# Modulation tiles moved between stages of a two-block transformer kernel, and fewer products for the second layer

## What is computed

```python
ctx_out = l < DEPTH - 1
m_lat = (silu_c @ w_mod[l] + b_mod[l]).reshape(Bsz, N_MOD, 1, D)
m_ctx = (silu_cc @ w_mod[l] + b_mod[l]).reshape(N_MOD, D)
x = x + 0.5 * m_lat[:, 2] * swiglu(modulate(rms_norm_2(x), m_lat[:, 0], m_lat[:, 1]), ffn_in[l, 0], ffn_out[l, 0])
...
x = x + m_lat[:, 5] * o_lat
x = x + 0.5 * m_lat[:, 8] * swiglu(modulate(rms_norm_2(x), m_lat[:, 6], m_lat[:, 7]), ffn_in[l, 1], ffn_out[l, 1])
if ctx_out:
    ctx = ctx + m_ctx[5] * o_ctx
    ...
```

## Time and profile before

| | |
|---|---|
| median of 3 runs | 2531.78 us (2530.11 to 2533.71) |
| the profiled execution | 2532.84 us, its span 2531.1 us |
| mean granted TensorE clock | 0.977 of full speed |
| PE busy | 2378.8 us, 94% |
| DVE busy | 1468.0 us, 58% |
| ACT busy | 919.6 us, 36% |
| first block | 0 to 484 us of the span |
| feed-forwards (0,0), (0,1), (1,0), (1,1) | from about 493, 1394, 1780 and 2322 us; some 350 to 385 us each, the last about 200 |
| layer 0's mixer and recurrence | about 865 to 1375 us |

### The profile page before, as it was taken

How to read it: one execution, slowest core, us unless ns; L and a number is a source line. 1 busy time by engine, 2 the same in 40 slices (tenths; PEclk the granted TensorE clock), 3 DMA queues, 4 the chain that set the end, 5 groups by cost and what they waited for, 6 DMA issues and landing times.

```text
span 2531.1 us, 43473 instructions
## 1 busy us (share of the span) xinstructions
PE 2378.8 (94%) x18326; PEld 1997.6 (79%) x18326; DVE 1468.0 (58%) x2431; ACT 919.6 (36%) x1582; POOL 76.5 (3%) x148
## 2 busy tenths in 40 slices
PE   8999899999999998887878999999999999999998
PEld 6678768788888776676766888888888888778997
DVE  5565566665555576767564655545655553575553
ACT  2341133432322447643324533222523222455542
POOL 0000000000000000000000000000000000000000
PEclk9999999999999999987989999999999999999999
DMA  8236525544444321000003344444344443213553
GB/s 308 100 103 231 183 100 178 171 133 150 144 148 154 124 84 51 1 3 4 21 4 117 109 150 139 144 143 166 118 148 150 142 151 124 87 34 103 183 185 130
DMA packets 55920, 311.01 MB, mean 123 GB/s; under 512 B 5936, under 2 KB 9392, under 8 KB 28080
## 3 DMA queue, kind: packets, MB, share of 16 engines
q1 hardware_dynamic: 32944, 224.75, 25.8%
q0 software_dynamic: 20736, 75.51, 9.1%
q10 hardware_dynamic: 2048, 7.98, 0.8%
HBM read 307.16 MB, written 1.05 MB: 122 GB/s over the span
## 4 chain that ended last, share of the span: by engine, by line
PE 80%; DVE 11%; ACT 5%; issue 3%; DVEq 0%; DMA 0%; ACTq 0%; SPq 0%
PE bank L1641 16%; PE bank L1648 16%; PE bank L1644 16%; PE bank L1464 5%; PE bank L1461 2%; PE bank L1523 2%; PE bank L1539 2%; PE bank L1737 2%; PE bank L1048 2%; PE bank L1275 1%; PE bank L1282 1%; PE bank L1278 1%; PE bank L1351 1%; PE bank L1583 1%; PE bank L1410 1%
## 5 line engine op out<-in xcount | busy, mean ns | idle before, releaser
L2774 DVE TENSOR_TENSOR w_lo<-ring,w_hi 128x1024 fp32r<-128x1024 f32 (+1 forms) x195 | 232.3, 1193 | 398.9 <-ACT w_hi L2224 398.9
L1641 PE MATMUL bank<-ffn_x_hi,w_hi 128*128 128x512 f32 x984 | 383.0, 389 | 0.0
L1644 PE MATMUL bank<-ffn_x_lo,w_hi 128*128 128x512 f32 x984 | 382.8, 389 | 0.0
L1648 PE MATMUL bank<-ffn_x_hi,w_lo 128*128 128x512 f32 x984 | 382.8, 389 | 0.0
L2224 ACT ACTIVATE w_hi<-ring 128x1024 fp32r<-128x1024 f32 (+1 forms) x195 | 200.2, 1028 | 275.5 <-PE bank L1644 242.4
L2692 DVE SCALAR_TENSOR_TENSOR ms<-mod_rows,c_silu 128x1024 f32<-128x1024 f32 x200 | 244.0, 1220 | 1.7
L1641 PEld LDWEIGHTS bank<-ffn_x_hi,w_hi 128*128 128x128 f32 x984 | 184.7, 188 | 38.7 <-DVE w_lo L2774 0.6
L1648 PEld LDWEIGHTS bank<-ffn_x_hi,w_lo 128*128 128x128 f32 x984 | 184.7, 188 | 38.3
L1644 PEld LDWEIGHTS bank<-ffn_x_lo,w_hi 128*128 128x128 f32 x984 | 184.7, 188 | 38.3
L1641 PE MATMUL bank<-ffn_h_hi,w_hi 128*128 128x512 f32 x484 | 190.2, 393 | 0.0
L1648 PE MATMUL bank<-ffn_h_hi,w_lo 128*128 128x512 f32 x484 | 188.3, 389 | 0.0
(11 more groups left out here) (523 smaller groups left out, 4975.7 us busy)
## 6 DMA issues: line engine op xcount, KB each, us to landing
ring<-in_stream SPq DMA_DIRECT2D x211, 1024.0 KB, 4.9
mod_rows<-in_mod_stream POOLq DMA_DIRECT2D x144, 512.0 KB, 3.8
one_const<-in_one ACTq DMA_DIRECT2D x1, 1665.0 KB, 13.5
mix_const<-in_two ACTq DMA_DIRECT2D x1, 1440.0 KB, 6.2
win_const<-in_win ACTq DMA_DIRECT2D x1, 1216.0 KB, 5.4
x<-in_x SPq DMA_DIRECT2D x4, 256.0 KB, 4.7
c_silu<-in_c SPq DMA_DIRECT2D x1, 1024.0 KB, 10.1
x<-in_x SPq DMA_DIRECT2D x1, 1024.0 KB, 26.0
```

What stands on the lines that cost most here:

```text
L1641: mm = pe.matmul(bank[:, 0:tok], w_high, hi, start=k == 0, stop=False)
L1644: mm = pe.matmul(bank[:, 0:tok], w_high, lo, start=False, stop=False)
L1648: mm = pe.matmul(bank[:, 0:tok], w_low, hi, start=False, stop=last)
L2774: V.tensor_tensor(low[:, 0:h.nk, :], raw_half(h), high[:, 0:h.nk, :].bitcast(F32), ALU.subtract).then_inc(sem("w_split"), 1)
```

## The change

The first block keeps 5 tiles in each layer instead of 11 (four beside v, one beside the embedding). The rest go to the four feed-forwards: 22, 19, 17 and 4 tiles. For vectors 5 to 8 of layer 1, the instructions for context tokens (parts 1 and 3) are left out, and bias and scale are applied to the latent column alone. DVE waits once more in layer 0's mixer, for its own last head norms.

```diff
-MOD_BLOCK_ONE = ([True] * 4 + [False, True, True, False] + [True, True, True, False] + [True, True, False, False]) * 2
-MOD_FFN = [True] * FF_IN_PAIRS + [False, True] * 5 + [True, False]
-MOD_PLAN = MOD_BLOCK_ONE + MOD_FFN + MOD_FFN + MOD_FFN[:-2]
-MOD_AFTER_SCAN = sum(MOD_BLOCK_ONE + MOD_FFN)
+MOD_BLOCK_ONE = ([True] * 4 + [False] * 4 + [True] + [False] * 7) * 2
+MOD_FFN = ([True] * FF_IN_PAIRS + [True] * 11 + [False], [True] * FF_IN_PAIRS + [False, True, True] * 4,
+           [True] * FF_IN_PAIRS + [False, True] * 6, [True] * 4)
+MOD_PLAN = MOD_BLOCK_ONE + sum(MOD_FFN, [])
+MOD_AFTER_SCAN = sum(MOD_BLOCK_ONE + MOD_FFN[0])
+assert sum(MOD_PLAN) == 2 * MOD_TILES
...
+            def layer_ends(layer, v):
+
+                return 1 if layer == 1 and v >= 5 else 2
+
...
-                    link(V.scalar_tensor_tensor(products[:].rearrange("p a b -> p (a b)"), mod_rows[:, part // 2, :], 1.0,
-                                                c_silu[:, part % 2, :], ALU.mult, ALU.mult, accum_out=dst))
+                    if part % 2 == 0 or layer_ends(layer, j // 4) == 2:
+                        link(V.scalar_tensor_tensor(products[:].rearrange("p a b -> p (a b)"), mod_rows[:, part // 2, :], 1.0,
+                                                    c_silu[:, part % 2, :], ALU.mult, ALU.mult, accum_out=dst))
...
-                done = modv[:, layer, v]
-                link(V.tensor_tensor(done, done, param("b_mod", 72 * layer + KC * v, KC).unsqueeze(2).broadcast_to([P, KC, 2]), ALU.add))
+                n = layer_ends(layer, v)
+                done = modv[:, layer, v, :, 0:n]
+                link(V.tensor_tensor(done, done, param("b_mod", 72 * layer + KC * v, KC).unsqueeze(2).broadcast_to([P, KC, n]), ALU.add))
...
+                if layer == 0:
+                    dve.wait_ge(sem("heads_plain"), 6)
                 last_unit = (1, 3, 5, 7) if layer else (3, 7, 9, 11)
```

## The result

The changed kernel takes 2540.89 us (median of 12 runs, 2536.48 to 2549.23); the kernel before, run beside it on the same chip, 2533.46 us (12 runs, 2528.91 to 2538.56). The ratio is 1.0032, with a 95% interval of 1.0019 to 1.0045: slower by 8.1 us (4.8 to 11.4) by the ratio, by 7.4 us in the medians. The forecast was 6.3 us. All ratios and medians here are of executions in the fast state; two executions of the kernel before that ran beside those of question 5 and the doubled tile took 5332 and 6996 us and are left out. The profiled execution of the changed kernel took 2536.48 us, its span is 2534.7 us.

A forecast was written before the change was run, and what follows sets the result against it. TensorE was taken as the bound (busy 94% of the span), VectorE's queue order setting only feed-forward ends and norm entries. Terms 0 + 0 + 0 + 0 + 6.3 + 0 gave +6.3 us, a median of 2538.1 us; range 2533.0 to 2543.0.

The forecast's parts named there:

- Part 5, the halt: End of feed-forward (0, 1): four products in the last slot delay the addition to x; TensorE halts 5.0 us (4.8 to 5.04).
- Part 5, the clock: Behind that halt: TensorE's work up to the second sum runs at lowered clock, 1.3 us more, at most 1.86.
- Parts 1 to 4: First block's relief, added head-norm wait, fewer instructions in (1, 0), fuller output halves of (0, 0) and (0, 1): 0 each.
- part 2: VectorE's added wait for its own head norms ahead of the multiplication by z: 0, or 0.22 us if uncovered.
- Part 1: First block: twelve tiles, 59 us of VectorE, leave; covered by TensorE's projections, so 0, at most 8.0 us gained.
- Part 6: Feed-forward (1, 1): four tiles, eight instructions, and row loads, hidden by 2.7 us in hand: 0, at most 10.1 us.
- A: End of (0, 1): the clock stays up and only the queue counts, +5.0 us, 2536.8 us; chance 0.15.
- B: First block gives back 2.7 us of lowered clock and waiting, so +3.6 us, 2535.4 us; chance 0.15.
- C: Faster: four instructions at the end of (0, 1) hidden, first block gives 8.0 us back, 2523.8 us; chance 0.05.
- D: (1, 1) falls behind as ACT and VectorE miss the 11.52 us round: up to 10.1 us more, 2548.2; chance 0.15.

The follow-up runs named there:

- question 5: Three runs: kernel before without layer 1's last context products, 2533.7 us; changed kernel with them kept, 2554.44; kernel before with twelve first-block tiles' products doubled, 2555.01.
- the doubled tile: Changed kernel with tile 50's four products, in the last slot of feed-forward (0, 1), done twice: ratio 1.0056 to the kernel before.
- the run with TensorE kept busy: Changed kernel with seven unneeded TensorE products of 384 columns in front of the sum at the end of (0, 1): 2536.86 us, ratio 1.0017.
- the run with twice the products there: Changed kernel with the context products of layer 1's last four vectors kept, so four products a group in (1, 1): 2554.44 us, ratio 1.0079.
- the one-multiplication kernel: Changed kernel with tile 50 one slot earlier and one unused 128x1024 VectorE multiplication in the last slot's place: ratio 1.0009 to the kernel before.

## Why the prediction was right, and where its sizes were off

**Verdict.** Slower was forecast and is what came; 2538.1 us stands against 2540.9, inside the range. Of the 2.8 us between them 1.7 are the kernel before, which itself ran at 2533.46 us beside these runs and not at 2531.78. The mechanism is the one named, at its place: four products between two splits, a wait of 4.86 us at the sum (4 to 5 said), lowered clock behind it, and the rest as before to within about 0.5 us.

**Part 5, the halt:** 5.0 us taken, 4.86 measured; 5.2 of the loss with the clock kept up. Right within the bounds said for the wait (4.8 to 5.04).

**Part 5, the clock:** this is the term that was mis-sized. I took 1.3 us, no more than the 1.86 us up to the second sum; it is 3.1, and part 5's sum of 6.3 us, bounded at 6.9, measured 8.3. Up to the second sum the two sums came 1.73 us further apart, so nearly all of that stretch ran slowly, not two thirds of it; that alone lies inside the bound of 1.86. Then I said that behind the second sum TensorE has room. It does not: the third group of sums is itself on the path to the norm, and a second fall slowed it, for 1.2 us that the sum put at nothing. That one shouldn't be put down to the change entirely, since it also stands in three profiles with little or no halt.

The Trainium skill (page "TensorE: Matmul & The Clock Gate", Terms) takes throttled time times one minus the ratio. From the four stretches above this is 5 x (0.50 + 0.17 + 0.15 + 0.19) = 5.05 us, where the run with TensorE kept busy gives 3.1: the trace doesn't agree, as it didn't in the earlier trace rows, and for the same reason, part of the low time is idle. Its sum in the prediction, 8.4 us, came nearer to the result than mine, but with a figure of another stretch that counted idle time and knew of no second fall: that was luck.

**Parts 1 to 4:** 0 each was taken, and the starts move by 0.2 us in all for the first block and (0, 0), within the 1 us said. The wait added in part 2 shows nowhere. Two small steps were overlooked by all six parts: some 0.3 us between 925 and 1000 us in layer 0's mixer, and some 0.25 us between 1380 and 1700 us. They stand in all ten profiles of kernels with the new places of the tiles and in none of the three with the old, so they are the change's. With the first goes, in the changed kernel from 865 to 1000 us, a wait of TensorE that the kernel before doesn't have there:

```profile
PE bank L1353 <- DVE mix_in_q L3032: 0.2, 1, 0.2
```

What makes them is open. Part 1 had a bound of 8 us of gain; none came.

**Part 6:** 0, and nothing new in the waits of (1, 1). It was the nearest call (2.7 us in hand, 2.3 used), and the run with twice the products there shows that the margin was read rightly, to 0.1 us of wait, though not what the waits cost (11.9 us, 8.7 expected).

**Rivals.** A (the clock stays up, +5.0) is excluded in all profiles with this halt; kept busy by hand, the kernel behaves as A said. B and C (something back from the first block) found nothing: its starts moved by 0.2 us. D, (1, 1) behind by up to 10.1 us, is what keeping the context products makes of it, and not what the change did.

The lower end of the range, 2533.0, is 0.4 us below what its own sum gives (2535.4 less 2); nothing hangs on it.

What stays open is why the second fall comes in some executions and not in others; with spare products in the halt it was absent once, which one profile doesn't settle.

## What to carry to other kernels

Off-path work in an in-order queue is free only as long as no critical instruction stands right behind it. Before filling a slot, look for the addition, split or copy that follows it, and for who reads that within the next microsecond. A fill plan deserves one look at its last slot before a norm.

Idle time in front of an instruction is no slack for it: the split had 4.12 us of idle time before it and 0.05 us behind it. Measure the slack from the end of the instruction to the start of its reader, and look when the data of the work put in would land.

Count a halt of TensorE that lowers its clock (those read here did so from 1.99 us on, those up to 1.64 us didn't, and those near 1.9 us at a norm's entry did so in some executions) as the halt plus the slow work behind it that is on the path, up to the next place with real room. And cover that is ample for a load says nothing of twice the load.

## What the runs showed of the hardware

At the end of (0, 1) the boundary grew by 3.1 to 3.4 us beyond the halt for halts of 2.08, 2.77, 4.86 and 5.27 us, and by 2.4 us for 9.92. Of each, 0.3 us is not the clock's. Two halts of 0.82 us left the clock up there, and six of 0.6 to 1.64 us did in (1, 1), while one of 1.99 us did not. Behind waits near 1.9 us at the entry of (1, 0) it fell in some executions and not in others. From 2.08 us on, the length of TensorE's halt did not raise the price; the work at 1.2 GHz behind it, on the path, made it.

And equal code shows falls of the clock in some executions and not in others: at 13 to 20 us, at 150 us and at the entry of (1, 0), each worth 1 to 4 us. In the recurrence the starts of two profiles differ by up to 10 us, and those of the one-multiplication kernel by 2.5. Not all of that is the clock: one of these profiles loses 4.6 us there against the kernel before, at the same granted clock (0.92 and 0.89 from 1000 to 1150 and from 1150 to 1375 us in both), and what it loses them to is open. The runs of one kernel differ by up to 14 us. In one profile such steps can hide or double an effect of 0.3%; comparing the starts of the same matmuls stage by stage separates them.
